# The RWKV pipeline of a hybrid decoder step, with its work in another order on every engine

## What is computed

```python
def rwkv7_mix(zb, prev_row, s0, mu, w0, w2, a0, a2, g2, k_k, k_a, r_k, ln_w, ln_b):
    ...
    w_log = -jax.nn.softplus(-(w0 + jnp.tanh(xw) @ w2)) - 0.5      # "lora" products and rates
    decay = jnp.exp(-jnp.exp(w_log))
    a = jax.nn.sigmoid(a0 + xa @ a2)
    g = jax.nn.sigmoid(xg) @ g2                                    # gate
    kk = heads(kf * k_k)
    kk = kk / jnp.maximum(jnp.sqrt(jnp.sum(kk * kk, -1, keepdims=True)), 1e-12)   # norm per head
    k_eff = heads(kf * (1.0 + (a - 1.0) * k_a))
    def step(S, inp):
        r_t, w_t, k_t, v_t, kk_t, a_t = inp
        sa = jnp.einsum('bhvk,bhk->bhv', S, kk_t)
        S = S * w_t[:, :, None, :] - sa[..., None] * (kk_t * a_t)[:, :, None, :] + v_t[..., None] * k_t[:, :, None, :]
        return S, jnp.einsum('bhvk,bhk->bhv', S, r_t)
    s_fin, y = lax.scan(step, s0, xs_t)
    y = (y - mean) * lax.rsqrt(var + GN_EPS) * ln_w + ln_b          # norm per head
    bonus = jnp.sum(rf * k_eff * r_k, -1, keepdims=True) * vf
    return (y + bonus) * g, s_fin, zb[:, -1]
```

## Time and profile before

| | us |
|---|---|
| median of 3 runs | 3706.42 |
| lowest and highest | 3706.07, 3719.03 |
| the profiled execution | 3703.33 |
| its span, first to last instruction | 3701.5 |
| PE busy | 3018.2 (82%) |
| DVE busy | 1440.2 (39%) |
| ACT busy | 853.7 (23%) |
| POOL busy | 338.4 (9%) |

### The profile page before, as it was taken

How to read it: one execution, slowest core, us unless ns; L and a number is a source line. 1 busy time by engine, 2 the same in 40 slices (tenths; PEclk the granted TensorE clock), 3 DMA queues, 4 the chain that set the end, 5 groups by cost and what they waited for, 6 DMA issues and landing times. The chain is left out here.

```text
span 3701.5 us, 55204 instructions
## 1 busy us (share of the span) xinstructions
PE 3018.2 (82%) x23634; PEld 2691.6 (73%) x23634; DVE 1440.2 (39%) x1961; ACT 853.7 (23%) x1527; POOL 338.4 (9%) x251
## 2 busy tenths in 40 slices
PE   2997787778588888989289999999540999999994
PEld 2996676766355556666189999999420999999993
DVE  3244343433433343420743333333578333333335
ACT  2112332321233333320321111111123111111111
POOL 0222323221000002300100000000101000000001
PEclk8997878785688898989689999999765999999996
DMA  2110000000100003630011111111050111111111
GB/s 91 40 45 10 2 2 2 2 13 3 50 1 7 9 0 140 211 143 23 0 52 45 45 41 44 45 40 45 6 23 9 49 45 45 40 45 45 44 41 48
DMA packets 53487, 147.34 MB, mean 40 GB/s; under 512 B 21840, under 2 KB 22224, under 8 KB 52464
## 3 DMA queue, kind: packets, MB, share of 16 engines
q1 hardware_dynamic: 44144, 107.73, 10.2%
q0 software_dynamic: 9216, 37.75, 2.9%
HBM read 137.95 MB, written 7.51 MB: 39 GB/s over the span
## 5 line engine op out<-in xcount | busy, mean ns | idle before, releaser
L395 PE MATMUL ps<-h_ffn,mlp_split 128*128 128x362 f32 (+1 forms) x4608 | 768.6, 329 | 65.1 <-DVE mlp_split L564 65.1
L395 PEld LDWEIGHTS ps<-h_ffn,mlp_split 128*128 128x128 f32 x4608 | 766.1, 190 | 67.1 <-issue 67.1
L395 PE MATMUL ps<-mlp_u,mlp_split 128*128 128x362 f32 (+1 forms) x4608 | 768.1, 328 | 11.1 <-DVE mlp_u L576 11.1
L395 PEld LDWEIGHTS ps<-mlp_u,mlp_split 128*128 128x128 f32 x4608 | 761.1, 189 | 15.8 <-DVE mlp_u L576 15.8
L582 DVE TENSOR_TENSOR y<-y,ps 128x362 f32<-128x362 f32 (+1 forms) x384 | 181.4, 528 | 466.6 <-PE ps L395 466.6
L535 ACT CAST mlp_split<-mlp_raw 128x1024 fp32r<-128x1024 f32 x128 | 134.2, 1049 | 619.7 <-PE ps L395 608.1
L574 DVE TENSOR_TENSOR mlp_relu<-mlp_relu 128x1088 f32<-128x1088 f32 x64 | 82.7, 1292 | 488.7 <-ACT mlp_relu L548 488.7
L395 PE MATMUL ps<-h,in_split 128*128 128x362 f32 (+1 forms) x1440 | 239.6, 329 | 33.8 <-POOL in_split L456 33.8
L395 PEld LDWEIGHTS ps<-h,in_split 128*128 128x128 f32 x1440 | 239.3, 190 | 34.8 <-issue 34.8
L248 POOL TENSOR_TENSOR x<-x,y 128x1088 f32<-128x1088 f32 x12 | 41.7, 3474 | 2048.0 <-DVE y L303 2048.0
L548 ACT ACTIVATE mlp_relu<-ps 128x362 f32<-128x362 f32 (+1 forms) x192 | 77.0, 475 | 531.2 <-PE ps L395 531.2
(11 more groups left out here) (382 smaller groups left out, 3829.0 us busy)
## 6 DMA issues: line engine op xcount, KB each, us to landing
mlp_raw<-w_mlp_dram SPq DMA_DIRECT2D x128, 512.0 KB, 3.5
in_raw<-w_in_dram SPq DMA_DIRECT2D x20, 512.0 KB, 3.5
x<-x_dram SPq DMA_DIRECT2D x2, 4352.0 KB, 14.8
y_dram<-x SPq DMA_DIRECT2D x1, 4352.0 KB, 11.7
out_ring<-w_out_dram SPq DMA_DIRECT2D x8, 512.0 KB, 4.1
pa_w<-w_pair_dram SPq DMA_DIRECT2D x4, 640.0 KB, 4.0
pa_rope<-rope_dram SPq DMA_DIRECT2D x1, 1088.0 KB, 6.5
ckv_dram<-z SPq DMA_DIRECT2D x1, 1088.0 KB, 8.8
```

Of the source, the lines that this page charges most:

```text
L395: last = self.nc.tensor.matmul(out, w[:, a, k, m], rhs[:, b, rk, at:at + c], start=(start and n == 0), stop=(stop and n == 2))
```

## The change

The lists of the four engines are put in another order, and the sums per head are computed the other way round.

- PE opens a turn with `lora(A)`, ahead of `weigh(C)`. `sigmoid_in`, which feeds it, moves to the end of the turn before on ACT, and `rates(A)` to the head of ACT's list; `decay(A)` opens DVE's list.
- `turn` is split. The transposes of value, kept key and `bp` are made a turn earlier, in stage A: the value behind the second `step`, the kept key behind `level_p` 3, `bp` behind `level_p` 4. Only `turn_kk` stays in stage B. Their copies (`v_out`, `k_out`, `b_out`) move between ACT's level copies.
- `gram_mb(B)` now stands ahead of `read_out(C)`, `gates(A)` between `read_out` and `gram_mk`, and `exps(A)`, `tanh_in(K)` ahead of `fresh(C)` on ACT. `key_sum(K)` moves from behind `level_x` 3 to behind `level_x` 2, `key_back(K)` from ahead of `level_p` 5 to behind it.
- The sums per head load the squares (128 by 128) as weights and stream a 2-column selector, so that tokens lie on partitions and the 8 heads along them. `key_inv` and `gn_inv` work on 128 by 8, then DVE writes each head's value 64 times (`widen`, 128 by 512), and `spread` multiplies that by the identity. The selector constants shrink from 544 columns to 2.

```diff
-                    def key_inv(j):
-                        n = key_n[:, 0:width(j)]
+                    def widen(to, of, j):
+                        w = slice(0, width(j))
+                        return nc.vector.tensor_copy(to[w, :, :], of[w, :].unsqueeze(2).to_broadcast([width(j), H, HD]))
+                    def key_inv(j):
+                        n = key_n[0:width(j), :]
                         wait("key_root", j)
                         link(ts(n, n, 1e-12, None, ALU.max))
-                        nc.vector.reciprocal(n, n).then_inc(g["key_inv"].sem, 1)
+                        link(nc.vector.reciprocal(n, n))
+                        widen(key_w, key_n, j).then_inc(g["key_inv"].sem, 1)
...
                     def key_sum(j):
                         wait("kk_sq", j)
-                        wait("rates", j - 1)
+                        wait("v_out", j - 1)
                         for p in range(PAIRS):
-                            end = mm(ps[0:H, 1, 0:width(j)], self.c("head_sel", lo=H * p, hi=H * p + H), nar(sq, j)[:, p, :], start=(p == 0), stop=(p == PAIRS - 1))
+                            end = mm(ps[0:width(j), 1, 2 * p:2 * p + 2], nar(sq, j)[:, p, :], self.c("head_sel"), start=True, stop=True)
...
                     def spread(to, of, j):
                         for p in range(PAIRS):
-                            end = mm(bank(to, PAIRS, width(j))[:, p, :], self.c("head_back", slice(0, H), lo=P * p, hi=P * p + P), of[:, 0:width(j)], start=True, stop=True)
+                            end = mm(bank(to, PAIRS, width(j))[:, p, :], of[0:width(j), 2 * p:2 * p + 2, :].rearrange("p a b -> p (a b)"), self.c("ident", slice(0, width(j)), hi=width(j)), start=True, stop=True)
...
+                    def turn_k(j):
+                        wait("bonus_v", j)
+                        wait("kp_in", j)
+                        turn(j, nar(kp, j), 0).then_inc(g["turned_k"].sem, 1)
...
                     def gram_mb(j):
-                        wait("turned_out", j, 3)
+                        wait("x_out", j - 1)
                         wait("kr_in", j)
+                        wait("bp_in", j)
```

More of the change, by code:

```diff
@@ L89, in constants @@
     put("head_mean", (s // HD == t // HD) / HD)
-    one = np.arange(H)
-    put("head_sel", np.concatenate([one[None, :] == 2 * p + np.arange(P)[:, None] // HD for p in range(PAIRS)], 1))
-    put("head_back", np.concatenate([one[:, None] == 2 * p + np.arange(P)[None, :] // HD for p in range(PAIRS)], 1))
+    put("head_sel", np.arange(P)[:, None] // HD == np.arange(2)[None, :])
     row, col = s % HD, np.arange(HD)[None, :]
@@ L855, in _ @@
                         if has(A):
-                            rates(A)
+                            gate_out(A)
+                            exps(A)
+                        if has(K) and K:
+                            tanh_in(K)
                         if has(C):
                             fresh(C)
-                        if has(A):
-                            gate_out(A)
                         if has(B):
@@ L1073, in gn_inv @@
                     def gn_inv(j):
-                        wait("gn_root", j)
-                        nc.vector.reciprocal(gn_n[:, 0:width(j)], gn_n[:, 0:width(j)]).then_inc(g["gn_inv"].sem, 1)
+                        wait("root", j)
+                        link(nc.vector.reciprocal(gn_n[0:width(j), :], gn_n[0:width(j), :]))
+                        widen(gn_w, gn_n, j).then_inc(g["gn_inv"].sem, 1)
                     def gn_out(j):
@@ L1118, in _ @@
                             level(B, 3)
+                        if has(K):
+                            key_inv(K)
                         if has(C):
@@ L1209, in _ @@
                             level_b(B, 2)
+                        if has(K):
+                            raw_key(K)
                         if has(A):
                             bonus_in(A)
-                            kept(A)
                         if has(B):
@@ L1459, in gn_sum @@
                     def gn_sum(j):
-                        wait("gn_sqr", j)
+                        wait("squared", j)
                         for p in range(PAIRS):
-                            end = mm(ps[0:H, 5, 0:width(j)], self.c("head_sel", lo=H * p, hi=H * p + H), nar(t2, j)[:, p, :], start=(p == 0), stop=(p == PAIRS - 1))
+                            end = mm(ps[0:width(j), 5, 2 * p:2 * p + 2], nar(t2, j)[:, p, :], self.c("head_sel"), start=True, stop=True)
                         end.then_inc(g["gn_sum"].sem, 1)
@@ L1474, in _ @@
                         if has(B):
-                            turn(B)
-                        if has(A):
-                            lora(A)
+                            turn_kk(B)
+                            gram_mb(B)
                         if has(C):
                             read_out(C)
+                        if has(A):
+                            gates(A)
                         if has(B):
-                            gram_mb(B)
+                            gram_mk(B)
                         if has(C):
@@ L1484, in _ @@
                         if has(B):
-                            gram_mk(B)
                             gram_a(B)
-                        if has(A):
-                            gates(A)
                         if has(C):
@@ L1507, in _ @@
                             level_x(B, 2)
+                        if has(K):
+                            key_sum(K)
+                        if has(B):
                             level_p(B, 3)
+                        if has(A):
+                            turn_k(A)
                         if has(C):
```

147 lines of the change are left out of this document (80 added, 67 removed).

## The result

| | before | after |
|---|---|---|
| time, median, us | 3711.45 | 3585.22 |
| profiled execution: time, span, us | 3703.3, 3701.5 | 3575.0, 3573.2 |
| turns 0 to 6 together, us | 424.8 | 313.0 |
| PE's waits in turns 0 to 6, us | 91.8 | 45.9 |
| PE busy in turns 0 to 6, us | 333.1 | 267.1 |

The ratio is 0.9657, with a 95% interval of 0.962 to 0.9694. The forecast was 3637 us with a range of 3585 to 3682, a gain of 69; measured is a gain of 126. The forecast started from a median of 3706.42, and beside the change the kernel before had 3711.45. Carried over to 3706.42 by the ratio, the time is 3579 us, just past the fast end of the range, and in the case to which the prediction gave a chance of 0.15.

The account below looks back on a forecast made before the run. PE bounds the stage: its list plus 13.1 us of waits a turn. A turn of 47.6 - 2.7 + 6.9 = 51.8 us, 8.9 less, gives 62 over seven; with 6.8 elsewhere, 69 us gained: 3637 us, range 3585 to 3682.

Parts of the forecast that it names:

- The waits: PE's waits in a full turn, walked in the new order: 6.9 us instead of 13.1, bounds 4 and 11.
- The clock: PE's busy time in a full turn falls by 2.7 us, a third of 8, as some 1.2 GHz stretches go.
- The gates' stretch stays: Of turn 3's five stretches at 1.2 GHz, the one at the gates remains; the other four, 17.4 us, stand behind vanishing waits.
- the thin sums: Two sums streaming hardly anything, in levels 2 to 3 and next to waits, were expected to cost the clock in some turns.
- turn 7: Its level products are half as many; the clock fell inside its levels for 87.6 us, taken as evidence for the changed levels.
- The price of a low stretch: Half of PE's busy time at 1.2 GHz: of 22.7 us in turn 3, about 11.3 us a turn.
- The clock holds throughout: Rival: busy time falls by all of 11.3 us, a turn is 43.2, the time 3577 us; chance 0.15.
- The falling clock: Rival: the clock falls in every turn's levels until the next turn's grams; 57.0 us a turn, 3673 us; chance 0.23.
- the lost clock: Rival: the clock never comes back, 1.2 GHz throughout; 76.6 us a turn, 3810 us; chance 0.06.
- The transposes: Moved into the levels, they count as work for the clock, as sixteen in a row were followed by 2.4 GHz.
- Outside the full turns: Gains of 2.6 us while the pipeline fills, 3.4 in turn 7 and 0.8 from smaller constants, together 6.8.
- The costs on DVE: Reciprocals fall from 0.94 to 0.15 us and `widen` adds 0.68: 0.1 us less each.

Follow-up runs that it names:

- lora_early: The kernel before with ScalarE's `sigmoid_in` moved to the end of the turn ahead, PE's order unchanged; 64 us faster than the kernel before, ratio 0.9827.
- thin_thrice: The change with the two-column products of `key_sum` and `gn_sum` issued three times each, same result; ratio 0.9805 to the kernel before, 76 us faster.
- transposes_thrice: The change with the transposes of v, k and b issued three times each, same result; ratio 0.9736 to the kernel before, 94 us faster.
- wide_thrice: The change with the sums of the kernel before, `key_sum` and `gn_sum` products issued three times each; ratio 0.976 to the kernel before, 85 us faster.

## Why the prediction was wrong

- **The waits: right.** Forecast 6.9 us a turn, measured 6.6. `lora` 0.8 (forecast 1.0), `step` 1.1 (1.2), `level_p` 1 to 5 0.5, 0.4, 0.5, 1.5 and 1.5 (0.5, 0.4, 0.5, 1.5, 1.5), `gn_back` 0 (0.3), `weigh` 0.1 (0), `key_back`, `transfer` and `gram_a` 0.
- **The clock: the step that failed.** The sentence was "I take a third of the 8 us, 2.7 (bounds +11.3 and, where it falls in every turn, -3)". Measured are 9.4 us a turn, from 47.6 to 38.2 busy. The mechanism was named rightly, that the low stretches stand behind waits that go; its size was not. Over seven turns the term is 66.0 us instead of 18.9, and these 47 are most of the 57 by which the gain was missed. Of the rest, 2 are waits, 2 lie outside the full turns, and the larger part is behind the stage, where the forecast counted no gain.
- **Why it was mis-sized.** Three readings went into it. "The gates' stretch stays" is refuted by lora_early, where the gates run at 2.4 GHz, behind the same wait of 0.9 us that the prediction held against the clock. That the thin sums would cost the clock in the levels is right in kind, since thin_thrice shows it, but wrong at their size: once each, the clock stays. And turn 7 was a poor model for the levels: its products are half as many, and turn 4's levels at 1.00 were the nearer rows; the prediction said so, and then took a middle.
- **The price of a low stretch** was put too high, at half of the busy time in it. The prediction's own row, `level_p` at 1.97 and 1.15 us, gives 0.42. By it the 22.7 us of turn 3 would have been worth 9.4 and not 11.3, and 9.4 is what a turn gave back on average.
- **The rivals.** "The clock holds throughout" came true: 44.7 us a turn, where it had worked out 43.2. That its time is so near, 3577 against 3579 on the same base, is luck: its turns were 10 us too short in all, and the 8 us behind the stage, which it did not count, make up for most of that. The falling clock and the lost clock didn't happen in turns 0 to 6, though turn 7 lost it, 22 us into the turn.
- **The transposes.** The reading that they count as work stands: sixteen of them and nothing else kept PE busy for 3.3 us, and 2.4 GHz came behind them. transposes_thrice agrees, where they cost 3 us a turn and left the clock at 0.98, but shows less by itself: twelve in a row take 1.5 us, about as long as the waits of 1.48 us that did not cost the clock either. Against this stands the rule of the Trainium skill that the prediction weighed (TensorE: Matmul & The Clock Gate, Part 4: PE-mode transpose), that the full clock doesn't engage for them. The trace disagrees, and it decides.
- **Outside the full turns.** Turn 7 gave 8.1 us instead of 3.4. Filling and constants together gave 0.4 instead of 3.4. PE waits 3.6 us less there, but it has more work ahead of the first `weigh` now (748 products instead of 720, and busy for 54.7 us instead of 51.5), which the walk through the filling turns left out.
- **The costs on DVE** were put a little too high: `widen` takes 0.43 us (forecast 0.68) and a reciprocal 0.20 (0.15), as these groups of the changed kernel show, and neither makes `key_back` or `gn_back` wait.

```profile
L915 DVE COPY rw_gn_w<-rw_gn_n 128x512 f32<-128x512 f32 x7 | 3.0, 428 | 0.2
L1097 DVE RECIPROCAL rw_gn_n<-rw_gn_n 128x8 f32<-128x8 f32 x7 | 1.4, 195 | 0.0
```

What stays open: how the gain of the clock is shared among the moves, since they don't add, how much of the last 16 us belongs to the transposes' places, and why turn 7 still loses the clock.

## What to carry to other kernels

Where the granted clock falls behind waits, first work out the turn at the full clock, as busy time less what the low stretches cost, plus the new waits, and forecast that unless some turn of the same shape shows a low clock with waits as short as the new ones. Take the cost of a low stretch from one group of products that the trace shows at both levels, and not as half. What a set of moves gives need not be the sum of what each gives alone: two waits of 3 us that stood one behind the other here gave back less clock together than one by one. To fill a wait, put one filler in each gap, as long as the gap; and where a filler is a run of products, look at the clock behind it, since a run of thin ones lost it here and a run of wide ones did not.

## What the runs showed of the hardware

- Twenty-four products with 128 columns of weights and two columns streamed kept TensorE busy for 2.84 us without a gap, and the clock fell to 1.2 GHz behind them (thin_thrice, 0.90 over the turns); the same number with 8 columns of weights and 128 streamed, 2.79 us, went with 0.96 (wide_thrice).
- A product of 128 rows and 128 columns of weights with two columns streamed takes as long as one with 8 columns of weights and 128 streamed: 1.05 and 1.04 us for eight.
- The clock's price of a longer wait at `lora` was 0.9 us for each us where it waited 1.8 us, and 1.3 where it waited 2.8, in one execution each; a `level_p` behind a wait of 1.48 us still took 1.15 us, as at 2.4 GHz.
- Sixteen transposes in a row, alone for 3.3 us at 1.2 GHz, were followed by 2.4 GHz.
